# Linear attention: the next head's decay moved into the chunks of the current head

## What is computed

```python
gate_logit = (gla_lr @ gla_gate_w2[l] + gla_gate_b[l])
log_a = jax.nn.log_sigmoid(gate_logit) / GLA_GATE_TAU
...
cum = jnp.cumsum(gi, axis=2)                       # the decay inside a chunk
o_inter = jnp.einsum('bhck,bhkv->bhcv', qi * jnp.exp(cum), state)
scores = jnp.einsum('bhik,bhjk,bhijk->bhij', qi, ki, decay)
...
state = state * exp(last) + (ki * exp(last - cum))^T vi
```

## Time and profile before

| | us |
|---|---|
| median of three runs | 2294.84 (2293.65 to 2296.45) |
| the profiled execution's own time | 2295.39 |
| its span, first to last instruction | 2293.4 |
| linear attention in it, first to last fill of G | 48.4 to 562.8 |
| first scores of heads 0, 1, 2, 3 | 130.53, 240.52, 352.06, 462.05 |

### The profile page before, as it was taken

The page is one execution under the profiler, slowest core; times in us unless marked ns, Lnnn a source line. Parts: engine busy times, 40 slices in busy tenths (PEclk is TensorE's granted clock), DMA queues, the critical chain, the costliest instruction groups (busy, mean ns, idle before and its releaser), DMA issues. The chain is left out here.

```text
span 2293.4 us, 29780 instructions
## 1 busy us (share of the span) xinstructions
PE 2131.7 (93%) x10088; PEld 1724.4 (75%) x10088; DVE 1287.4 (56%) x1744; ACT 757.0 (33%) x1326; POOL 921.2 (40%) x733
## 2 busy tenths in 40 slices
PE   4999989998999999999999699997799999999999
PEld 3787777777877777777877478886688888888887
DVE  4557676852275675675676466557544444444444
ACT  3223232321154454454454420002422222223322
POOL 3322222222244344344344233332855555555552
PEclk7999999999899999999999799998799999999999
DMA  3211111222414314314324172221111111111111
GB/s 104 48 34 46 28 46 30 49 48 78 99 29 101 78 41 101 78 41 101 78 41 110 70 270 74 91 83 46 56 56 44 37 47 55 55 55 55 55 55 73
DMA packets 137775, 153.84 MB, mean 67 GB/s; under 512 B 7664, under 2 KB 112112, under 8 KB 137728
## 3 DMA queue, kind: packets, MB, share of 16 engines
q1 hardware_dynamic: 136000, 150.07, 23.8%
q10 hardware_dynamic: 1728, 3.15, 0.4%
HBM read 107.06 MB, written 20.97 MB: 56 GB/s over the span
## 5 line engine op out<-in xcount | busy, mean ns | idle before, releaser
L123 POOL TENSOR_TENSOR w_hi<-w_raw,w_ones 128x64 fp32r<-128x64 f32 x88 | 34.2, 389 | 763.7 <-PE gla_g L147 362.2
L478 POOL TENSOR_TENSOR sb_rows<-sb_beta,sb_rest 128x128 f32<-128x128 f32 (+7 forms) x128 | 166.1, 1302 | 250.8 <-DVE sb_rest L833 250.8
L833 DVE TENSOR_TENSOR_SCAN sb_rest<-sb_rest 128x128 f32<-128x128 f32 (+7 forms) x128 | 205.6, 1614 | 33.6 <-ACT sb_beta L684 33.6
L126 POOL TENSOR_TENSOR w_lo<-w_raw,w_hi 128x1024 fp32r<-128x1024 f32 x88 | 218.5, 2483 | 7.3
L839 DVE TENSOR_TENSOR sb_wt_lo<-sb_t,sb_wt_hi 128x512 fp32r<-128x512 f32 x192 | 106.4, 554 | 172.3 <-ACT sb_wt_hi L692 170.3
L692 ACT CAST sb_wt_hi<-sb_t 128x512 fp32r<-128x512 f32 x192 | 92.6, 482 | 234.0 <-PE sb_t L577 232.8
L147 PE MATMUL sb_g<-h_hi,w_hi 128*128 128x512 f32 x544 | 161.1, 421 | 3.7 <-DVEq L737 3.7
L147 PE MATMUL sb_g<-h_lo,w_hi 128*128 128x512 f32 x544 | 156.3, 413 | 0.0
L147 PE MATMUL sb_g<-h_hi,w_lo 128*128 128x512 f32 x544 | 153.1, 406 | 0.0
L147 PE MATMUL gla_g<-h_hi,w_hi 128*128 128x512 f32 x480 | 132.1, 408 | 1.8 <-DVEq L1251 1.8
L577 PE MATMUL sb_t<-ident,sb_rows 128*128 128x128 f32 x576 | 102.4, 289 | 32.1 <-DVE sb_wt_lo L839 32.0
(11 more groups left out here) (310 smaller groups left out, 5084.6 us busy)
## 6 DMA issues: line engine op xcount, KB each, us to landing
w_raw<-w_in SPq DMA_DIRECT2D x64, 512.0 KB, 8.1
ff_raw_g<-w_ffn_gate SPq DMA_DIRECT2D x11, 1024.0 KB, 5.4
ff_raw_u<-w_ffn_up SPq DMA_DIRECT2D x11, 1024.0 KB, 5.8
ff_raw_d<-w_ffn_down SPq DMA_DIRECT2D x11, 1024.0 KB, 4.9
sb_qs<-sb_q_st SPq DMA_DIRECT2D x32, 256.0 KB, 5.1
sb_kh<-sb_k_st SPq DMA_DIRECT2D x32, 256.0 KB, 5.1
sb_kl<-sb_k_st SPq DMA_DIRECT2D x32, 256.0 KB, 5.0
mp_sig<-gates_t SPq DMA_DIRECT2D x16, 512.0 KB, 4.4
```

Source lines behind the costliest of these rows:

```text
L123: self.nc.gpsimd.tensor_tensor(hi[:, 0:64], raw[:, 0:64], self.ones[:], ALU.mult)
L126: self.nc.gpsimd.tensor_tensor(lo, raw, hi, ALU.subtract).then_inc(self.ready, 1)
L478: nc.gpsimd.tensor_tensor(rows[tb // 4][:, tb % 4, 0:width], beta[:, n % 2, 0:width], rest[:, n % 2, 1:width + 1], ALU.mult).then_inc(row_ ...
L833: nc.vector.tensor_tensor_scan(back, back, back, 1.0, ALU.mult, ALU.bypass).then_inc(scanned, 1)
```

## The change

The logits of the next head are made in slots 6 and 9, one half each, in `G[0]` and `G[1]` between the unit q and the unit k. ScalarE takes absolute values, exponential and logarithm in slots 7, 10, 13 and 16, VectorE the minimum in 7 and 10, the subtraction in 19 and the cumulative sum in 22; they work in a new buffer `decay` and no longer in `E`. `transpose_o` and `gate_o` move by one slot (28 to 31), in the last head too, and `transpose_v` and `copy_v` by one (34 to 37). `exponential` is now in the slots of `EXP_SLOT`; VectorE's nine exponents and factors begin in slot 29 and, from slot 31 on, stand behind one another. Each G bank has one use more in a head, so `g_uses` grows by 7, and `use_of` counts units around it.

```diff
@@ -888,6 +888,10 @@
 GLA_TASKS = 9
 GLA_T = CHUNKS + 8
 GLA_CHAIN = 13
+O_SLOT = (28, 29, 30, 31)
+V_SLOT_GLA = (34, 35, 36, 37)
+LOGIT_SLOT = (6, 9)
+EXP_SLOT = (26, 30, 32, 35, 37, 38, 40, 41, 43)
 N_MADE = 3 + 3 * (LEVELS - 1) + 1
 
 
@@ -909,6 +913,7 @@
         q_in, k_out = sb("q_in", [P, S]), sb("k_out", [P, S])
         C = sb("c", [P, S])
         E = sb("e", [P, 2, S])
+        decay = sb("decay", [P, 2, S])
         dec = sb("dec", [P, CHUNKS])
         vt = sb("vt", [P, 2, S])
         V = sb("v", [P, CHUNKS, GLA_DV])
@@ -948,9 +953,11 @@
         gate_out = [sem(f"gate_out{h}") for h in range(NH)]
         dve_step = sem("dve_step")
 
-        g_uses = lambda it: 7 + GLA_UNITS * it
+        g_uses = lambda it: 7 + (GLA_UNITS + 1) * it
+        use_of = lambda it, n: g_uses(it) + n + (n > 0)
+        abs_uses = lambda prep: 2 + 3 * (prep - 1)
         t_uses = lambda it: 4 + GLA_T * it
-        s_uses = lambda it: 1 + (CHUNKS + 1) * it
+        s_uses = lambda it: 1 + CHUNKS * it
         N_LAST_GATES = 6
 
         def blocks(t, half):
@@ -1016,9 +1023,10 @@
 
                 def body(it, last):
                     for n in range(GLA_UNITS):
-                        W.split(pool, GLA_UNITS * it, GLA_UNITS + n, (g_done[1], GLA_UNITS * it + (GLA_UNITS + n)))
+                        freed = g_uses(it) + (n - 1 + (n > 2 and not last))
+                        W.split(pool, GLA_UNITS * it, GLA_UNITS + n, (g_done[1], freed))
                 rounds(pool, GLA_HEADS, body)
-                W.split(pool, GLA_TILES, 0, (g_done[1], GLA_TILES))
+                W.split(pool, GLA_TILES, 0, (g_done[1], g_uses(GLA_HEADS - 1) + GLA_UNITS - 1))
 
             @block.tensor
             def _(pe):
@@ -1049,6 +1057,12 @@
                         at = slice(half * HALF, (half + 1) * HALF)
                         ins = nc.tensor.matmul(flat[:, at], w2_h[:], lr_t[:, at], start=True, stop=True)
                     ins.then_inc(s_done, 1)
+
+                def next_logits(prep, half, use):
+                    pe.wait_ge(w2_ready, prep + 1)
+                    pe.wait_ge(g_free[half], use + 1)
+                    at = slice(half * HALF, (half + 1) * HALF)
+                    nc.tensor.matmul(G[half][:], w2_h[:], lr_t[:, at], start=True, stop=True).then_inc(g_done[half], 1)
 
                 def low_rank():
 
@@ -1114,17 +1128,19 @@
                             scores(it, s // 3)
                         if s < 3 * CHUNKS and s % 3 == 2:
                             outputs(it, s // 3)
-                        if s in (27, 28, 29, 30):
-                            transpose_o(it, s - 27)
+                        if s in O_SLOT:
+                            transpose_o(it, O_SLOT.index(s))
                         if not last:
-                            if s == 25:
-                                logits(it + 1, s_uses(it) + CHUNKS)
-                            if s in (33, 34, 35, 36):
-                                if s == 33:
+                            if s in LOGIT_SLOT:
+                                next_logits(it + 1, LOGIT_SLOT.index(s), g_uses(it) + 1)
+                            if s in V_SLOT_GLA:
+                                n = V_SLOT_GLA.index(s)
+                                if n == 0:
                                     for half in range(NH):
-                                        pe.wait_ge(g_free[half], g_uses(it) + 5)
-                                transpose_v(s - 33, t_uses(it) + CHUNKS + 4 + s - 33)
-                        fill(GLA_UNITS * it, GLA_UNITS + s // 8, s % 8, g_uses(it) + s // 8)
+                                        pe.wait_ge(g_free[half], use_of(it, 3) + 2)
+                                transpose_v(n, t_uses(it) + CHUNKS + 4 + n)
+                        fill(GLA_UNITS * it, GLA_UNITS + s // 8, s % 8,
+                             g_uses(it) + s // 8 if last else use_of(it, s // 8))
                 rounds(pe, GLA_HEADS, body)
 
             @block.scalar
@@ -1158,6 +1174,20 @@
                     nc.scalar.activation(e, e, ACT.Exp, scale=-1.0).then_inc(abs_ready, 1)
                     act.wait_ge(abs_ready, 2 * prep + 2)
                     nc.scalar.activation(e, e, ACT.Ln, bias=1.0).then_inc(log_ready, 1)
+
+                def next_abs(prep, half, use):
+
+                    act.wait_ge(g_done[half], use + 1)
+                    nc.scalar.activation(decay[:, 0, half * HALF:(half + 1) * HALF], G[half][:], ACT.Abs, bias=gb_h[:]
+                                         ).then_inc(abs_ready, 1)
+
+                def next_exp(prep):
+                    act.wait_ge(abs_ready, abs_uses(prep) + 2)
+                    nc.scalar.activation(decay[:, 0, :], decay[:, 0, :], ACT.Exp, scale=-1.0).then_inc(abs_ready, 1)
+
+                def next_log(prep):
+                    act.wait_ge(abs_ready, abs_uses(prep) + 3)
+                    nc.scalar.activation(decay[:, 0, :], decay[:, 0, :], ACT.Ln, bias=1.0).then_inc(log_ready, 1)
 
                 def exponential(prep, task):
                     act.wait_ge(d_ready, GLA_TASKS * prep + task + 1)
@@ -1219,29 +1249,34 @@
                                     act.wait_ge(g_free[half], g_uses(it) + 1)
                             sigmoid_r(s // 4)
                         if not last:
+                            if s in (7, 10):
+                                next_abs(it + 1, s // 10, g_uses(it) + 1)
+                            if s == 13:
+                                next_exp(it + 1)
+                            if s == 16:
+                                next_log(it + 1)
                             if s in (20, 24, 28, 32):
                                 i = (s - 20) // 4
                                 if i == 0:
                                     act.wait_ge(r_ready, 2 * (it + 1))
-                                copy_vt(i // 2, i % 2, g_uses(it) + 2 + i // 2)
-                            if s == 26:
-                                log_sigmoid(it + 1, s_uses(it) + CHUNKS)
-                            if s in (33, 34, 35, 36):
-                                copy_v(s - 33, t_uses(it) + CHUNKS + 4 + s - 33)
-                            if s in (31, 32, 34, 37, 38, 39, 41, 42, 43):
-                                exponential(it + 1, (31, 32, 34, 37, 38, 39, 41, 42, 43).index(s))
+                                copy_vt(i // 2, i % 2, use_of(it, 2 + i // 2))
+                            if s in V_SLOT_GLA:
+                                n = V_SLOT_GLA.index(s)
+                                copy_v(n, t_uses(it) + CHUNKS + 4 + n)
                             if s in (36, 40, 44):
                                 i = (s - 36) // 4
                                 if i == 0:
                                     act.wait_ge(o_out, 16 * 4 * (it + 1))
-                                copy_r(i // 2, i % 2, g_uses(it) + 4 + i // 2)
+                                copy_r(i // 2, i % 2, use_of(it, 4 + i // 2))
+                            if s in EXP_SLOT:
+                                exponential(it + 1, EXP_SLOT.index(s))
                         elif s >= 4 and s % 4 == 0:
                             i = s // 4 - 1
                             send_gate(i // 2, i % 2, g_uses(it) + i // 2)
                     if last:
                         send_gate(N_LAST_GATES - 1, 1, g_uses(it) + N_LAST_GATES - 1)
                     else:
-                        copy_r(1, 1, g_uses(it) + 5)
+                        copy_r(1, 1, use_of(it, 5))
                 rounds(act, GLA_HEADS, body)
 
             @block.vector
@@ -1281,6 +1316,22 @@
                     chain.link(nc.vector.tensor_tensor(e1, e1, e0, ALU.subtract))
                     nc.vector.tensor_tensor_scan(C[:], keep[:], e1, 0.0, ALU.mult, ALU.add).then_inc(d_ready, 1)
                     dve.wait_ge(d_ready, GLA_TASKS * prep + 1)
+
+                def next_min(prep, half, use):
+
+                    dve.wait_ge(abs_ready, abs_uses(prep) + half + 1)
+                    dve.wait_ge(g_done[half], use + 1)
+                    nc.vector.tensor_scalar(decay[:, 1, half * HALF:(half + 1) * HALF], G[half][:], gb_h[:], 0.0,
+                                            ALU.add, ALU.min).then_inc(g_free[half], 1)
+
+                def next_decay(prep, use):
+                    dve.wait_ge(log_ready, prep + 1)
+                    for half in range(NH):
+                        dve.wait_ge(g_free[half], use + 2)
+                    chain.link(nc.vector.tensor_tensor(decay[:, 1, :], decay[:, 1, :], decay[:, 0, :], ALU.subtract))
+
+                def next_scan(prep):
+                    nc.vector.tensor_tensor_scan(C[:], keep[:], decay[:, 1, :], 0.0, ALU.mult, ALU.add).then_inc(d_ready, 1)
 
                 def exponents(prep, task):
 
@@ -1383,28 +1434,37 @@
                             gate_r(it, s // 3)
                         if s == 25:
                             normalise(it)
-                        if s in (27, 28, 29, 30):
```

(42 more changed lines are left out.)

## The result

The changed kernel took 2269.56 us (median of four runs, 2264.57 to 2274.35) against 2294.24; the ratio is 0.9898, 95% interval 0.988 to 0.9916, so 23 us less by the ratio and 24.7 between the medians. Forecast: 2273.5, range 2266 to 2282. One of the ten executions of e_scan_late took 2692.84 us at a granted clock of 0.742, where every other one of it shows 0.966 to 0.974, and is left out of its ratio.

What follows compares the result with a forecast made beforehand. VectorE's chain, started late by the decay behind the last gate, was taken to end three stretches. Terms -17.5 (stretches less logits), -2.8 (clock), -1.4 (head 3) make -21.7 from 2295.39; forecast 2273.5 us, range 2266 to 2282.

Steps and rivals of the forecast that it cites:

- Three stretches: Behind the chunks of heads 0 to 2: each falls from 50.25 to 42.5 us, 7.75 saved per head.
- Logits in the chunks: Chunks 2 and 3: the four logits matmuls moved there lengthen the chunks by 1.9 us a head.
- Clock given back in the chunks: Chunks of heads 1 and 3: shorter waits ahead spare clock falls, 2.8 us back (bounds 0 and 2.8).
- Head 3: Last head, no logits or sum: transposes one slot later cut the 3.12 us wait by one portion, 1.36 us.
- the last meeting with GpSimd: End of VectorE's chain: 1.47 us for 0.69; stretch 42.85 us with it, 42.0 if missed, taken as 42.5.
- may cost a fall, hidden mostly behind VectorE: Output transposes: the new 2.4 us wait may lower TensorE's clock, mostly hidden behind VectorE's work.
- The 43.1: Stretch length if a meeting with GpSimd cost the whole 2.71 us and the 0.8 seen, instead of 42.5.
- GpSimd's split: VectorE's chain: the split behind the fourth unit newly falls on it, plus 2.9 us (bounds 2.2 and 3.5).
- The wait at the output transposes: Heads 0 to 2: TensorE's wait of 1.03 us there grows to about 2.4 us.
- TensorE is not the bound: Judges the rival that TensorE bounds the stretches: 40.95 us each, 2268.5 us in all, chance 0.17.
- ScalarE's queue: Rival: late exponentials delay copies, TensorE and VectorE wait for one another; stretch near 45 us, 2283.5 in all, chance 0.2.
- The projection bank: Rival, chunks 2 and 3: unit k waits for logits, absolute value and minimum; slower, 2303 us, chance 0.03.

Runs made afterwards that it cites:

- e_scan_late: Changed kernel with subtraction, cumulative sum and first exponents and factors put back behind the output gates; 2290.8 us, ratio 0.9994 to the kernel before.
- e_chain_plus: Changed kernel with one unread 128x1024 product added to VectorE's chain behind the gates; 2274.88 us, ratio 0.9928 to the kernel before.
- e_short_lo: Changed kernel with GpSimd's long subtraction in the linear attention cut to 64 of 1024 weight columns; 2259.42 us, ratio 0.9862 to the kernel before.
- e_scan20: Changed kernel with the next head's cumulative sum in slot 20 instead of 22; 2266.41 us, ratio 0.9877 to the kernel before.
- e_slots_only: Kernel before with only output transposes, gates, and transposes and copies of v one slot later; 2310.03 us, ratio 1.0071.
- e_late29: Changed kernel with output transposes, those of v and exponentials one slot later still; 2268.04 us, ratio 0.9887 to the kernel before.
- both kernels of 6 and 9: Changed kernel with sum in slot 20 and transposes and exponentials one slot later, run twice: 2262.98 us, ratio 0.988; 2264.86 us, ratio 0.9871.
- e_early27: Changed kernel with output transposes, those of v, VectorE's steps and exponentials one slot earlier, decay still early; 2279.32 us, ratio 0.9932 to the kernel before.

## Why the prediction was right

**The bound** (VectorE's chain behind the gates, started late by the cumulative sum) is shown from both sides: put the sum and the two tasks that need it back and the gain is gone (e_scan_late), lengthen the chain and the stretch follows (e_chain_plus), shorten it enough and TensorE ends the stretch (e_short_lo). The waits for v left with it.

**The terms.** Three stretches: forecast -23.3, measured -22.8. Logits in the chunks: +5.7, measured +5.3 (1.7 in head 0, 1.8 in head 2 at equal clock). Clock given back in the chunks: -2.8, measured -2.7 (the four chunk stretches together are 2.6 us longer than before: 5.3 of logits less 2.7). Head 3: -1.4, measured 43.63 to 42.30. Sum of these -21.7 forecast and -21.5 measured. The other 2.2 us of the 23.7 in the spans lie outside: 0.5 ahead of the first scores and 1.7 behind the linear attention, where nothing was changed and which varies by more from run to run. These are the profiled executions; the median of the changed kernel lies 2 us under its profiled one.

**The step that was mis-sized** is within the first term, twice, with opposite signs. The stretch was forecast at 42.5 and took 41.61 at full clock: 9.73 to the transposes instead of 9.95, the last gate's end 6.9 after the first transposes instead of 7.1 (201.28 to 208.14 in e_scan20, where no clock fell), and the last meeting with GpSimd was missed, which I had counted half (the chain of 24.98 us is the 25.65 of the forecast, 22.75 + 2.9, less the 0.8 of that meeting). Against that, "may cost a fall, hidden mostly behind VectorE" was wrong: the fall behind the 2.2 us wait costs 1.6 us in full (43.20 and 43.16 against 41.61). It hits the output transposes, which the gates wait for, so it is ahead of VectorE's chain and not beside it. That the term came out at -22.8 is luck: three times 0.9 too long, 2.7 us, against two falls of the clock, 3.2 us; the same kernel had only one fall in its second trace. TensorE had not 1.5 us in hand but 0.7. (The 43.1 that the prediction gives for dearer meetings does not follow from its own terms; no other number hangs on it.)

**GpSimd's split** was right in kind: two meetings of 3.0 and 3.1 us in the chain, 2.9 forecast (the one around 213.42 spreads three operations from 210.75 to 216.23, 5.5 us, where elsewhere their like start 1.25, 0.61 and 0.60 apart). A third lies in `normalise`, before the change as well; the prediction priced only what the later start adds to it (0.6 with the sum, 0.44 measured), not the meeting itself, of which e_short_lo takes away 2.1 us. Which engine is held depends on which starts first: in e_slots_only the subtraction starts at 207.65 and the sum, 1.0 behind it, takes 4.32 us for 2.29, while in the kernel before the sum starts at 208.94 and GpSimd's conversion, 0.12 behind it, takes 2.96 us for 1.00:

```profile
209.06 2.96 POOL L124 TENSOR_SCALAR w_hi<-w_raw 128x960 fp32r<-128x960 f32 x1
```

The Trainium skill's rule ("SBUF — State Buffer", "Who interferes with whom": a VectorE instruction with two SBUF inputs and a GpSimd instruction that reads SBUF get in each other's way, and issue order decides which one blocks) is borne out by these rows and by e_short_lo.

**The wait at the output transposes.** Forecast 2.4, measured 2.2, and 0.44 of it is the sum in slot 22 (e_scan20).

**Rivals.** TensorE is not the bound, but the margin is thin: 0.7 us of last wait was left, and 41.61 less 0.73 is 40.9, what the prediction had for TensorE alone (40.95). Only without its wait at the transposes does it come down to 38.65 (e_short_lo). ScalarE's queue passed nothing on in the changed kernel (no wait for `gla_v`); it does as soon as VectorE comes later, 0.6 us in e_chain_plus and 3.6 to 4.2 in e_scan_late. The projection bank did not block: no wait ahead of slots 8 and 12.

## What to carry to other kernels

When an engine ends a stretch, work of it that depends on nothing in that stretch is worth moving. It brings more than its length: what needs it can fill earlier holes (here the first `exponents` and `factors`, 1.22 us each between the gates), and what stands queued behind it on other engines is freed (here ScalarE's copy of v). Put it into a hole of that engine, not ahead of the next thing others wait for: slot 20 and slot 22 differ by 0.4 us a head, and in these traces by whether the clock falls. A second change can be worth something only beside the first: the moved slots cost 16 us alone and bring 8 with the early decay. Ask of a wait left on TensorE whether what follows it is on the chain, for then a fall of the clock is paid in full (1.6 us here).

## What the runs showed of the hardware

TensorE's granted clock fell from 1.00 (2.4 GHz) to about half of it (1.2 GHz) behind some waits and not behind others of the same length. Of nine waits of 2.20 to 2.22 us (changed kernel twice, e_chain_plus) six were followed by a fall; of waits of 1.8 us and less at the same place, none (e_scan20, e_late29, both kernels of 6 and 9); of the four waits of 3.1 to 3.6 us in e_early27, all; of the seven of 2.85 to 3.29 us in the kernel before, four; of the six of 5.3 to 6.2 us in e_slots_only, all. In e_scan_late one of four waits of 1.97 to 1.98 us was followed by a fall (0.72 over the next 2.7 us). This chance may be part of why the changed kernel's runs lie 10 to 13 us apart; how much of that, and what makes the 1721 to 1730 us of the unchanged part vary, the runs don't tell.
